# 32 of 96 modulation tiles moved between the expert-gate groups, gates on three PSUM pairs

## The reference

```
# product-key experts (first block)
act = einsum('tkd,td->tk', expert_down[idx], h)       # 128 chosen experts a token
w   = gate * gelu(act)                                # gate: softmax over the chosen
out = einsum('tk,tkd->td', w, expert_up[idx])
# modulation of the second block: two layers, two condition vectors
mod = silu(c) @ w_mod + b_mod                         # two layers, two vectors; w_mod: 2 x 2048 x 6144
```

## Time and profile before

| | us |
|---|---|
| median of three runs | 4051.4 |
| the three runs | 4050.0, 4051.4, 4071.2 |
| profiled execution | 4045.6 |
| its span | 4043.8 |

### The profile page before, as it was taken

How to read it: one execution, slowest core, us unless ns; L and a number is a source line. 1 busy time by engine, 2 the same in 40 slices (tenths; PEclk the granted TensorE clock), 3 DMA queues, 4 the chain that set the end, 5 groups by cost and what they waited for, 6 DMA issues and landing times.

```text
span 4043.8 us, 73486 instructions
## 1 busy us (share of the span) xinstructions
PE 3846.4 (95%) x30344; PEld 3566.3 (88%) x30344; DVE 2409.5 (60%) x3400; ACT 1673.4 (41%) x2349; POOL 818.0 (20%) x599
## 2 busy tenths in 40 slices
PE   6999998899999988999999999999999999989997
PEld 6767677799999987999999999999799997778887
DVE  6999976543677767555555555533333333657556
ACT  4223345544455567333444334432222223243674
POOL 4878763234400000000000000000000002113223
PEclk9999999999999999999999999999999999999999
DMA  5777773245455544555655555522522223214323
GB/s 218 300 305 276 302 283 133 108 180 185 168 191 193 195 140 137 190 197 188 225 221 217 194 201 194 191 105 95 175 91 86 104 104 125 94 66 143 116 104 135
DMA packets 141589, 695.06 MB, mean 172 GB/s; under 512 B 44256, under 2 KB 54624, under 8 KB 61664
## 3 DMA queue, kind: packets, MB, share of 16 engines
q1 hardware_dynamic: 89952, 641.77, 43.2%
q10 hardware_dynamic: 51456, 50.74, 3.7%
HBM read 672.54 MB, written 19.92 MB: 171 GB/s over the span
## 4 chain that ended last, share of the span: by engine, by line
PE 77%; DVE 14%; ACT 3%; issue 3%; DMA 1%; POOL 1%; ACTq 0%; DVEq 0%; SPq 0%; POOLq 0%
PE banks L422 50%; PE banks L2231 17%; DVE w_lo L400 2%; PE banks L2299 1%; DVE pq L1340 1%; DVE banks L1330 1%; PE banks L2142 1%; PE banks L2401 1%; ACT w_hi L392 1%; DVE rq L1376 1%; DVE banks L1317 1%; DVE oh L1577 1%; PE banks L2467 1%; PE banks L2442 1%; POOL w_lo L400 1%
## 5 line engine op out<-in xcount | busy, mean ns | idle before, releaser
L422 PE MATMUL banks<-h_hi,w_hi 128*128 128x256 f32 (+1 forms) x6176 | 1640.7, 287 | 62.4 <-DVE w_lo L400 30.8
L422 PE MATMUL banks<-h_hi,w_lo 128*128 128x256 f32 (+1 forms) x6176 | 1617.3, 283 | 0.0
L422 PE MATMUL banks<-h_lo,w_hi 128*128 128x256 f32 (+1 forms) x6176 | 1616.9, 283 | 0.0
L392 ACT CAST w_hi<-ring 128x1024 fp32r<-128x1024 f32 x986 | 984.4, 1048 | 1041.3 <-PE banks L2231 427.5
L400 DVE TENSOR_TENSOR w_lo<-ring,w_hi 128x1024 fp32r<-128x1024 f32 x806 | 1000.8, 1274 | 559.7 <-ACT w_hi L392 555.2
L422 PEld LDWEIGHTS banks<-h_hi,w_hi 128*128 128x128 f32 x6176 | 1110.7, 189 | 126.3 <-issue 98.5
L422 PEld LDWEIGHTS banks<-h_hi,w_lo 128*128 128x128 f32 x6176 | 1109.4, 189 | 13.2 <-issue 0.5
L422 PEld LDWEIGHTS banks<-h_lo,w_hi 128*128 128x128 f32 x6176 | 1109.1, 189 | 11.8
L400 POOL TENSOR_TENSOR w_lo<-ring,w_hi 128x1024 fp32r<-128x1024 f32 x180 | 460.3, 2557 | 1628.9 <-ACT w_hi L392 1627.4
L2231 PE MATMUL banks<-wp_hi,w_hi 128*128 128x256 f32 x2048 | 566.3, 277 | 5.2 <-DVE wp_lo L1610 5.1
L2231 PE MATMUL banks<-wp_hi,w_lo 128*128 128x256 f32 x2048 | 566.1, 276 | 0.0
(11 more groups left out here) (388 smaller groups left out, 4307.3 us busy)
## 6 DMA issues: line engine op xcount, KB each, us to landing
ring<-in_stream_dram SPq DMA_DIRECT2D x555, 1024.0 KB, 4.8
spare<-in_stream_dram SPq DMA_DIRECT2D x30, 1024.0 KB, 5.9
cst<-in_stream_dram SPq DMA_DIRECT2D x23, 1024.0 KB, 6.7
g_in<-g_out ACTq DMA_DIRECT2D x8, 1024.0 KB, 6.4
g_out<-stage ACTq DMA_DIRECT2D x31, 256.0 KB, 2.6
hb<-heads_d ACTq DMA_DIRECT2D x8, 768.0 KB, 6.7
heads_d<-stg ACTq DMA_DIRECT2D x4, 1024.0 KB, 8.7
X<-in_x_in_dram SPq DMA_DIRECT2D x2, 1024.0 KB, 7.1
```

The source lines that it names most:

```text
L392: act.copy(w_hi[:, t.par, s], weights(t.slot)[:, s]).then_inc(hi_done, 1)
L422: m = pe.matmul(bank(b, e - a, a), w[:, t.par, k], x(k)[:, a:e], start=first and a == 0, stop=last and e == n, skip_group_check=e - a < n)
```

## The change

32 of the 96 modulation tiles leave the mix stage and form a phase "gmod" of their own between "down0" and "up0". A chunk of the mix stage keeps eight of its twelve modulation tiles and two blocks for three. Blocks 16 to 23 are made in the gate groups: after group n PE has made min(32, 32(n+1)//28) tiles. The late condition vectors and the copied block lie where constants for a later stage were. Gate groups turn over three pairs of banks, since bank 7 is needed for the blocks and bank 6 for their turns; PE therefore waits for group n-3. ACT and DVE loops over the groups are written out. The first tile of "up0" is split after the groups. The bias of the second layer is added after the "up0" stage's rounding.

```diff
-PHASES = [("u", 8), ("v", 4), ("mix", 136), ("gate", 12), ...
-          ("down0", 64), ("up0", 64), ("down1", 64), ("up1", 64),
+PHASES = [("u", 8), ("v", 4), ("mix", 104), ("gate", 12), ...
+          ("down0", 64), ("gmod", 32), ("up0", 64), ("down1", 64), ("up1", 64),
-SLOTS = [(D_, M_, M_), (M_, M_), (D_, M_), (D_, M_), (M_, M_), (D_, M_), (D_, M_), (M_, M_)]
+SLOTS = [(D_, M_), (M_,), (D_, M_), (D_, M_), (M_,), (D_, M_), (D_, M_), (M_,)]
+LATE = 16
-LAST = {4: G0["gate"], 5: G0["mix"] + MIX * 6 + 4, 6: G0["mix"] + MIX * 4 + 11}
+LAST = {4: G0["gate"], 5: G0["mix"] + MIX * 6 + 3, 6: G0["mix"] + MIX * 4 + 9}
         def gate_banks(n):
-            b = 2 * (n % 4)
+            b = 2 * (n % 3)
+        def late_by(n):
+            return min(32, 32 * (n + 1) // 28)
...
 (ACT, gate groups)
+            def late_out(b):
+                act.wait_ge(mm_done, Tile("gmod", 4 * (b - LATE) + 3).done())
+                act.wait_ge(S("mod_turned"), b)
+                act.copy(mtmp_late, bank(7)).then_inc(S("mod_out"), 1)
+            gates_weigh(0)
+            gates_weigh(1)
+            blocks = LATE
+            for n in range(2, 32):
                 gates_weigh(n)
+                gates_stage(n - 2)
+                if n >= 3:
+                    gates_store(n - 3)
+                while blocks < 24 and late_by(n - 1) >= 4 * (blocks - LATE + 1):
+                    late_out(blocks)
+                    blocks += 1
+            hi_split(act, Tile("up0", 0))
             for n in range(30, 32):
                 gates_stage(n)
                 gates_store(n - 1)
             gates_store(31)
+            act.wait_ge(S("mod_turned"), 24)
+            act.copy(modf[:, 8 * LATE:], bank(6, 64)).then_inc(S("mod_read"), 1)
...
 (DVE, gate groups)
+            for n in range(2, 32):
+                onehots(n)
+                scale(n - 2)
             scale(30)
             scale(31)
+            for h in (1, 0):
+                lo_split(dve, Tile("up0", 0), h)
...
 (PE, gate groups)
-                if i is not None or n >= 4:
-                    pe.wait_ge(S("gates_in"), g(-3))
-                    pe.wait_ge(S("g_staged"), g(-3))
+                if n >= 3:
+                    pe.wait_ge(S("gates_in"), g(-2))
+                    pe.wait_ge(S("g_staged"), g(-2))
...
+            def late_tile(j):
+                t = Tile("gmod", j)
+                if j % 4 == 0:
+                    pe.wait_ge(S("mod_out"), LATE + j // 4)
+                pe.wait_ge(tile_loaded[t.slot], t.loaded())
+                for r in range(4):
+                    m = pe.matmul(banks[32 * r:32 * r + 32, 7, :], csp_late[:, 4 * (j % 4) + r], weights(t.slot)[:, 4 * r:4 * r + 4],
+                                  start=(j % 4 == 0), stop=(j % 4 == 3))
+                m.then_inc(mm_done, 1)
+            def late_turn(b):
+                pe.wait_ge(S("mod_out"), b + 1)
...
+            turned, made = LATE, 0
+            for n in range(32):
                 gates_pe(n)
+                if turned < 24 and made >= 4 * (turned - LATE + 1):
+                    late_turn(turned)
+                    turned += 1
+                while made < late_by(n):
+                    if made % 4 == 0 and made // 4 + LATE > turned:
+                        late_turn(turned)
+                        turned += 1
+                    late_tile(made)
+                    made += 1
+            while turned < 24:
+                late_turn(turned)
+                turned += 1
+            pe.wait_ge(S("mod_read"), 2)
             up_pe(0)
```

More of the change, by code:

```diff
@@ L50 @@
 D_, M_ = True, False
-SLOTS = [(D_, M_, M_), (M_, M_), (D_, M_), (D_, M_), (M_, M_), (D_, M_), (D_, M_), (M_, M_)]
-MIXED = {"mix": [t for slot in SLOTS for t in slot]}
+SLOTS = [(D_, M_), (M_,), (D_, M_), (D_, M_), (M_,), (D_, M_), (D_, M_), (M_,)]
+MIXED = {"mix": [t for slot in SLOTS for t in slot], "gmod": [M_]}
+LATE = 16
 MIX = len(MIXED["mix"])
@@ L730, in _ @@
                     down_act(t, i * 4 + (j + 4 * SELECT))
+            for j in range(60, 64):
+                t = Tile("down0", j)
+                if j < 63:
+                    hi_split(act, t.next())
+                down_act(t, j)
             act.sem_inc(S("sel_acts"), 1)
@@ L778, in _ @@
             gates_store(31)
+            act.wait_ge(S("mod_turned"), 24)
+            act.copy(modf[:, 8 * LATE:], bank(6, 64)).then_inc(S("mod_read"), 1)
             act.dma_start(C("rm"), consts[:, CONST["rm"][0]:CONST["rm"][0] + 1024]).then_inc(S("back"), 16)
             act.dma_start(C("rg"), consts[:, CONST["rg"][0]:CONST["rg"][0] + 512]).then_inc(S("back"), 16)
-            up_act(0)
+            for j in range(4):
+                hi_split(act, Tile("up0", j).next())
+            up_act(0, 1)
             act.wait_ge(mm_done, G0["down1"])
@@ L1380, in heads_scaled, with bias @@
                     .then_inc(S("qk_ready"), 1)
+            def bias(layer):
+                L(dve.tensor_tensor(mods[:, layer], mods[:, layer],
+                                    V("bmod", 48 * layer, 48).unsqueeze(2).to_broadcast([P, 48, 2]), ALU.add))
             for j in range(12):
@@ L1395, in _ @@
                     dve.wait_ge(S("mod_read"), 1)
-                    for layer in range(2):
-                        L(dve.tensor_tensor(mods[:, layer], mods[:, layer],
-                                            V("bmod", 48 * layer, 48).unsqueeze(2).to_broadcast([P, 48, 2]), ALU.add))
+                    bias(0)
             dve.wait_ge(S("back"), 16)
@@ L1635, in _ @@
             up_dve(0)
+            dve.wait_ge(S("mod_read"), 2)
+            bias(1)
             for layer in range(2):
@@ L2049, in mod_turn @@
                 for n in range(4):
[L2050 removed]
+                    m = pe.matmul(bank(b // 2 % 2, 2, T + 8 * b + 2 * n), mtmp[:, n * P:(n + 1) * P], C("pick", 0, 2), start=True, stop=True)
                 m.then_inc(S("mod_turned"), 1)
@@ L2244, in up_pe @@
                     tile(j, None, 60)
-            for n in range(4):
-                gates_pe(n)
-            with pe.Fori(0, 7, 1) as i:
-                for n in range(4, 8):
-                    gates_pe(n, i, 4)
+            def late_tile(j):
[9 more added lines that the diff above has]
+                pe.wait_ge(S("mod_out"), b + 1)
+                for n in range(4):
+                    m = pe.matmul(bank(6, 2, 8 * (b - LATE) + 2 * n), mtmp_late[:, n * P:(n + 1) * P], C("pick", 0, 2),
+                                  start=True, stop=True)
+                m.then_inc(S("mod_turned"), 1)
+            pe.wait_ge(S("mix_in"), 3)
+            turned, made = LATE, 0
+            for n in range(32):
+                gates_pe(n)
+                if turned < 24 and made >= 4 * (turned - LATE + 1):
[11 more added lines that the diff above has]
+            pe.wait_ge(S("mod_read"), 2)
             up_pe(0)
```

52 lines of the change are left out of this document (20 added, 32 removed).

## The result

| | before | after |
|---|---|---|
| median of five runs, us | 4053.8 | 4128.1 |
| lowest and highest, us | 4050.0, 4071.2 | 4113.1, 4168.1 |
| profiled execution, us | 4045.6 | 4168.1 |
| its span, us | 4043.8 | 4166.3 |

The changed kernel takes 1.0175 times as long (95% interval 1.014 to 1.021), 74 us between the medians. The forecast was 4079 us in a range of 4054 to 4112 us: slower, as said, but by nearly three times as much, and outside the range. Of the rivals it is B (stores come late, 4117 us) that comes nearest.

The account below looks back on a forecast made before the run. The prediction took DVE to bound the steady mix chunks and transfers to bound the changed gate groups. Mix stage -4.5, groups +30 and tail +2 gave +27.5 us on 4051.4 us: 4079 us, range 4054 to 4112 us.

Parts of the forecast that it names:

- rival B: Gate groups: stage copies wait for stores landing after 5.2 us, +68 us there, +65 us in all, 4117 us; chance 0.18.
- What bounds each stage: DVE sets the steady mix chunks at 61.1 us; in the gate groups TensorE alone would need 3.26 us a group.
- rival C: Mix stage: TensorE sets it, so all 38 us of its shed work would come off; chance 0.08.
- Transfers set the groups, +30 us: Gate groups: loads and stores need 3.85 us of all transfer engines per group, more than TensorE's 3.26 us; +30 us.
- I take 0.93: Gate groups: share of full transfer use assumed, turning 97.7 us of transfers into 105 us, +30 us instead of +22.
- Its threshold (landing of 3.9 us): Gate groups: late stores decide from a landing of about 3.9 us on; up to there loads hold the groups.
- The page on queues: Transfer engines alternate between queues by whole packets, so a store would wait for one or two packets of loads.
- Mix stage, -4.5 us: Mix stage with 32 tiles fewer: steady chunks gain 0, last two chunks and the end gain 4.5 us, bounds 1 and 9.
- Three bank pairs, 0: Gate groups: TensorE's tighter wait, for group n-3 instead of n-4, costs 0.
- Tail, +2 us: After the last gate group: the next stage's first tile is split there, no longer ahead; +2 us, bounds 0 and 5.
- Sum: Whole kernel: -4.5 + 30 + 2 = +27.5 us, 4079 us from the median of 4051.4 us.

Follow-up runs that it names:

- early: The changed kernel with ACT's copy out of a chunk's first modulation block moved to right after the fourth dense tile's read; 4121.0 us, 1.0163 of before.
- noload: The changed kernel with its 32 late products made from weight tiles already in the ring, nothing loaded between the groups; 4071.6 us, 1.0037 of before.
- nostore: The changed kernel without the 32 stores of the groups' results and the stage copies' waits for them; 4078.6 us, 1.0044 of before.
- stage4: The changed kernel with four stage buffers instead of two, same bytes stored and loaded; 4101.2 us, 1.0112 of before.
- best: The changed kernel with four stage buffers, stores in 2 KB pieces and ACT's first block copy moved earlier; 4075.4 us, 1.0055 of before.
- after_again: The changed kernel run and profiled once more with no edit; median 4137.5 us, 1.0183 of before.
- pairs3: The kernel before with only the three bank pairs, written-out group loops and ACT staging two groups earlier, no tile moved; 4049.9 us, 0.9964 of before.
- before_again: The kernel before run and profiled once more with no edit; ratio 1.0023 to its own kernel.

## Why the prediction was off

- *What bounds each stage.* Right. Mix chunks stayed 61.10 us, so rival C (TensorE sets the mix stage) is out; and in early, with the wait for the copy gone, the stage ended 2 to 3 us sooner than before, not 38. In the groups TensorE's own period was right to within a microsecond (105.5 us in noload and nostore).
- *Transfers set the groups, +30 us.* This is the step that failed. Its size, 3.85 us of transfer work per group at 0.93 of full use, agrees with the length of stage4 (124.5 us, share 0.95), though there too the waits were on stores and not on loads, and best moved the same bytes at the same share in 107.9 us. But the kernel has two stage buffers, and with two ACT never offers the transfers enough work: share 0.74, +68 to +71 us. The words that failed are "I take 0.93". The doubt that use would fall short was put down to TensorE's order of late tiles and priced at 5 us more; the tighter link (store, landing, stage copy, next store) stood further down as rival B.
- *Rival B.* Its mechanism was right, and so was its price, 26 groups x 2.6 us = 68 us; but that the price fits this closely is luck. It took every store to land after 5.2 us and every group to be 2.6 us longer. What came were medians of 3.2 and 4.2 us with single landings of 13 to 15.5 us: 15 to 17 waits of 54 to 57 us in all, on top of the 11 us that TensorE's work costs. The rival had 0.18 because of one argument: "once the groups are that slow, the loads need only 70% of the time and are out of the stores' way". The chain refutes it: landings of 5.7 to 15.5 us at a share of 0.74. That share is a mean of full and half-empty slices (the row in tenths above), so a store can still meet loads, and here each delay goes straight into the period, since only half a microsecond of slack was there. Its threshold (landing of 3.9 us) was passed by the median in after_again (4.2 us) and not in the first profile (3.2 us): half of the stores there land in time, the others very late, and those set the stretch.
- *The page on queues.* The rule of the Trainium skill (DMA: Bandwidth & Descriptors, Queues, rings and completion order) that the engines alternate between queues by whole packets leant to rival B. The runs go that way, with landings rising from 2.6 us (noload) to medians of 3.2 to 7.9 us beside loads; they don't show that the alternation is the reason.
- *Mix stage, -4.5 us.* Wrong, most likely in sign: about +3 us (+4.1 between the first profiles, where the first gate tile starts at 590.18 for 586.11; +2.7 between the medians of the last turn). The sign is not beyond doubt, since pairs3, with the mix stage of before, comes as late as 588.6; that 4.5 us were not gained is clear. Each term was an effect of less work, and none asked whether ACT's written order still met the new order of TensorE. It didn't: TensorE waited 40.8 us in the stage for block copies queued behind casts and tables. Most of it lay beside DVE's work, some 3.7 us did not. The gain without that is about 1 us, a quarter of the forecast and at its lower bound. Which of its terms was too high isn't shown; none of them allowed for the clock, which was 0.93 to 0.95 in the lighter stage for 0.97 to 0.99.
- *Three bank pairs, 0.* Right, at least in the groups (pairs3: 92.6 us).
- *Tail, +2 us.* Right: 4.1 us from the last product to "up0" against 1.9 to 2.0. The row 1669.79 above is the split, two halves in 2.35 us, that the forecast had moved there.
- *Sum.* With rival B's price for the groups and the measured terms for the rest it is +68 +3 +2 = 73 us, 4127 us from the new median of before, 4053.8.

## What to carry to other kernels

Before transfers are put beside a stage that stores its results, write down the slack of each buffer: here a landing of 2.6 us against one group's period of 2.87 us. If the slack is less than a landing may grow when it meets loads (here to 8 us in the median and 20 at most), deepen the buffers first; with four of them, +70 us became +30, and with stores in larger pieces and loads spread evenly, +7. Look also at what stands between a store and its data in the engine's order: here each store stood behind the stage copy of the next group, which waits for the landing of the store before, so two buffers gave only one store under way. Moving the store ahead of that copy costs no buffer; no run here tried it. When the work of one engine in an order written out by hand is thinned, follow each hand-over block by block on the other engines: a lighter engine arrives earlier at places where the others are as late as ever.

## What the hardware showed unexpectedly

The dense products of 256 columns run at one of two paces at the same granted clock. View by stretches of 50 us in "up0", first after, then after_again; both are nothing but L2261 products, with the granted clock at 1.00:

```profile
1700.00:1750.00 50.00, 50.00 (x427) 50.00 (x426) 26.85 (x36) 17.78 (x18) 0.00 (x0) 1.00 0.52 183
```

```profile
1700.00:1750.00 50.00, 50.00 (x444) 50.00 (x443) 28.78 (x38) 18.67 (x19) 0.00 (x0) 1.00 0.54 194
```

427 products in 50 us are 0.117 us each, 444 are 0.113 us, 4% apart. The same program has either pace in the same place in two executions; a pace often holds for hundreds of microseconds, and where it was looked at closely it changed where TensorE paused, if only for 0.02 to 0.3 us (in after at about 1437, in noload at about 1135). In the first profile of after the slow pace held from about 1050 to 1437 us and from 1673 us through "up0" and "down1" to about 2400: 28 us more in "up0" to "up1" than before. It is not in the three profiles of kernels without late tiles (before twice, pairs3) at these places; of the ten with them, seven have it somewhere between "up0" and "up1". Whether the change makes it likelier is left open. The difference of the medians needs no share of it.

The stage with the gated linear units ran at a granted clock of 0.99 in the first profile of before and at 0.94 in its second, where the stretch around it was 10 us longer (904.0 against 893.8 us above); that the clock is the whole of the 10 us isn't shown. The rows of before_again and after_again for 690 to 850 us:

```profile
690.00:850.00 160.00, 136.02 (x961) 125.51 (x960) 84.97 (x159) 86.00 (x150) 40.92 (x17) 0.94 0.33 119
```

```profile
690.00:850.00 160.00, 135.81 (x967) 125.37 (x966) 86.24 (x162) 88.15 (x154) 40.86 (x17) 0.95 0.33 114
```

So two single profiles can be tens of microseconds apart in places that no edit touched (45 us between the first ones of before and after), and stretches are to be compared, not spans.
